# Other PSUM banks for the recurrent block's gate and input tiles, and each modulation tile one place earlier

## The chip, the core and the metric

The kernel runs on one core of a Trainium2 chip. The metric is the device time of one execution in microseconds (us). The core has five engines that run side by side and meet only at semaphores: TensorE (PE, matrix products, with weight loads as PEld), VectorE (DVE), ScalarE (ACT), GpSimd (POOL) and SyncE (SP, which issues most DMAs). PE writes its products into PSUM, which has 8 banks of 128 x 512 fp32 values; DVE and ACT read them there.

## The reference, cut to what matters

Two transformer-like blocks of one layer each run over 512 tokens of width 1024. The first (`first_block`) has latent attention, a Fourier branch, gates and 16 experts. The second (`second_block`) has a gated recurrence, a short convolution and a feed-forward part.

```
mod_l = s_lat @ w_mod + b_mod                 # shift, scale, gate: 6 x 1024
h = modulate(rms(x), sh1, sc1);  p = h @ w_in
ga, gb = sigmoid(p[GA]), sigmoid(p[GB])
x = x + g1 * (ga * (attn @ w_o) + gb * (fourier @ w_fourier)) @ w_out
x = x + g2 * expert_choice(modulate(rms(x), sh2, sc2))
# second block
z = rms(x) @ w_in_2 -> lru_x, lru_gate, sc_b, sc_c, sc_x
lru_x = causal_dwconv(lru_x); r, i = sigmoid(lru_x @ wa), sigmoid(lru_x @ wx)
y_lru = scan(a(r), sqrt(1 - a^2) * i * lru_x) * gelu(lru_gate)
y_sc = sc_b * causal_dwconv(sc_c * sc_x)
x = x + concat(y_lru, y_sc) @ w_out_2
x = x + (gelu(conv(h @ w_gate)) * conv(h @ w_up)) @ w_down;  out = rms(x)
```

## The kernel before

Activations are kept transposed: 128 channels on the partitions, 512 tokens along the free dimension, so that one PSUM bank holds one tile of 128 channels. Each fp32 product of the projections is made of three products: the operands are split into a high and a low part, and `mm3` (lines 959 to 963) issues high x high (L961), low x high (L962) and high x low (L963). `project` runs `mm3` over the contraction blocks, 8 of them for an input of 1024, so a tile is 24 matmuls. Weights arrive in chunks of 128 x 2048; ACT writes their high part (L1704) and POOL their low part (L895).

The order on each engine is the order of the code. Which bank a tile goes to is settled by a plan that is made before the program is built (`make_plan`). Each `p.add(name, by=..., bank=...)` enters a tile in the order in which PE will open it. Its bank is the one given, or the next of the list that the last `p.phase(n, banks)` set. The plan also notes which tile held that bank before, and which event frees it (`by`). On PE, `open_tile` (line 935) waits for that event before the tile's first matmul. So the plan does not move an instruction; it decides what PE waits for at the head of each tile.

Three places matter here.

**Gate projections and modulation.** The tiles `ga` 0 to 7 and `gb` 0 to 7 are projections of 24 matmuls each (lines 1180 to 1185). Between them PE runs `mod_b_tile(k)`, k = 0 to 15: two products with one column, which sum over partitions what DVE has made in `macc`. `mod_b_tile` waits for `macc_done` k + 1 (line 996). On DVE, `modulation_b(c)` (line 2100) multiplies one chunk of modulation weights, 8 instructions long, the last of which (L2112, into `macc`) signals `macc_done`. `modulation_b(0)` starts when the query rows are finished (`qtok_done` 8). DVE does `modulation_b` 0 to 3, and then always one `mod_b_evac(c)` (L2097) and `modulation_b(c + 4)`. In the kernel before, `mod_b` 0 stands behind `ga` 4, `mod_b` 4 behind `gb` 0, and `mod_b` 12 to 15 behind `four_o` 0 to 3.

**Input and gate tiles of the recurrence.** PE makes `lru_x` 0 to 7, each of 24 matmuls, and behind `lru_x` 3, 4, 5, 6 and 7 the small products of the gates (`lru_r` and `lru_i`, lines 1537 and 1540): those of index 0; 1 and 2; 3; 4; 5. Tiles 6 and 7 follow behind `sc_c` 0. DVE takes each `lru_x` with `lru_conv(j)`: L2627, L2633, twice L2636, and L2638, which signals `conv_done` j + 1 and frees the bank of `lru_x` j. Ahead of it, from j = 3, comes `lru_gates(j - 3)` on DVE (L2643), which waits for ACT's sigmoid of `lru_i`.

**The recurrence's output gates and `mix_o`.** PE makes `lru_gate` 0 to 7, one after the other. Each is scaled on DVE (L2689), passed through a gelu on ACT (L2016), multiplied on DVE (L2694), split into its high part on ACT (L1714) and its low part on DVE (L2075), and only this last instruction frees its bank. Then `project_two` opens `mix_o` 0 and `mix_o` 1 together, before the first matmul of either, and runs 12 blocks of both: four of the short convolution, then eight of the recurrence.

In the kernel before `lru_x` 5 goes to the bank of `lru_x` 2, `mix_o` 0 to that of `lru_gate` 2, and `mix_o` 1 to that of `lru_gate` 3.

Of the kernel before, what the change touches and what calls it, by code (L numbers as in the profile page):

```python
# [33 lines left out]
LRU = 8  # L34
# [16 lines left out]
B = 128  # L51
# [151 lines left out]
def blocks(base, first, count, width=B):  # L203

    return range(base + first // CH, base + (first + count * width - 1) // CH + 1)


def split_steps():

    o = Order()  # L210
    for j in range(KD):
        o.add("h", j)
    for j in range(KD):
        o.add("hc", j)
    o.add("f", 0)
    o.add("f", 1)
    for j in range(QL):
        o.add("cq", j)
    for j in range(KL):
        o.add("ckv", j)  # L220
    o.add("f", 2)
    o.add("f", 3)
    for g in range(NF + 1):
        if g < NF:
            o.add("f_ch", g, 0)
            o.add("f_ch", g, 1)
        if g >= 1:
            o.add("four", g - 1)
    for h in range(H):
        o.add("q", h)  # L230
        o.add("k", h, 0)
        o.add("k", h, 1)
    for j in range(4):
        o.add("attn", j)
    for j in range(KD):
        o.add("m", j)
    for i in range(PAIRS):
        o.add("ye", i, 0)
        o.add("ye", i, 1)
    for j in range(KD):  # L240
        o.add("g", j)
    for j in range(SC):
        o.add("y_sc", j)
    for j in range(LRU):
        o.add("y_lru", j)
    for j in range(KD):
        o.add("g2", j)
    for q in range(QUARTERS):
        for i in range(FQ):
            o.add("ff", q, i)  # L250
    return o


SPLITS = split_steps()
# [7 lines left out]
PRE_FF = PRE_SC + SC + LRU  # L262
GATES_AFTER = {3: (0,), 4: (1, 2), 5: (3,), 6: (4,), 7: (5,)}
GATES_LAST = (6, 7)
X_BANKS = (3, 4, 0, 1, 6, 0, 1, 6)
R_BANKS = (2, 2, 3, 2, 2, 2, 2, 3)
I_BANKS = (5, 7, 4, 3, 5, 7, 0, 1)


SQ0 = 5 + QL + KL + 1  # L270
# [10 lines left out]
def make_plan():  # L281
    p = Plan()
# [37 lines left out]
    for half in range(2):  # L320
        for t in range(TT):
            p.add("uq", half, t, by=("qtok_done", half * TT + t + 1), bank=half * TT + t,
                  split=[c for k in range(QL) for c in blocks(s1, q_block(half, k), 1, QW)])
    p.phase(6)
    for j in range(KD):
        p.add("ga", j, by="act", split=blocks(s1, S1_GA + j * 8 * B, 8))
        if j >= 4:
            p.add("mod_b", j - 4, by=("modb_done", j - 3))
    for j in range(KD):
        p.add("gb", j, by="act", split=blocks(s1, S1_GB + j * 8 * B, 8))  # L330
        p.add("mod_b", 4 + j, by=("modb_done", 5 + j))

    def four_o(j, bank=None):
        p.add("four_o", j, by=("resid_done", j + 1), split=blocks(s1, S1_FO[j], NF), bank=bank)

    for j in range(KD // 2):
        four_o(j)
        p.add("mod_b", 12 + j, by=("modb_done", 13 + j))
    for t in range(KT):
        p.add("uk", t, by=("ktok_done", t + 1), split=blocks(s1, S1_K, 8), bank=t)  # L340
    for t in range(KT):
# [80 lines left out]
    w = SPLIT0["w_in_2"]  # L422

    def lru_gates(i):
        p.add("lru_r", i, by="act", bank=R_BANKS[i])
        p.add("lru_i", i, by=("lru_b_done", i + 1), bank=I_BANKS[i])

    for j in range(LRU):
        p.add("lru_x", j, by=("conv_done", j + 1), split=blocks(w, j * 8 * B, 8), bank=X_BANKS[j])
        for i in GATES_AFTER.get(j, ()):  # L430
            lru_gates(i)
    for j in range(SC):
        if j == 1:
            p.phase(6, (2, 0, 3, 1, 4, 5))
        p.add("sc_c", j, split=blocks(w, (LRU + 3 * j) * 8 * B, 8), bank=4 if j == 0 else None)
        if j == 0:
            for i in GATES_LAST:
                lru_gates(i)
        p.add("sc_x", j, split=blocks(w, (LRU + 3 * j + 1) * 8 * B, 8), bank=5 if j == 0 else None)
        p.add("sc_b", j, by=("lo_done", SPLITS["y_sc", j] + 1), split=blocks(w, (LRU + 3 * j + 2) * 8 * B, 8),  # L440
              bank=6 if j == 0 else None)
    for j in range(LRU):
        p.add("lru_gate", j, by=("lo_done", SPLITS["y_lru", j] + 1), split=blocks(w, (LRU + 3 * SC + j) * 8 * B, 8))
    for j in range(KD):
        p.add("mix_o", j, by=("resid_done", RES2 + j + 1), split=blocks(SPLIT0["w_out_2"], j * 12 * B, 12),
              bank=(5, 2, 0, 3, 1, 4, 1, 4)[j])
    w = SPLIT0["ffn"]
    p.phase(5)
    for q in range(QUARTERS):
# [6 lines left out]


PLAN = make_plan()
TILE = PLAN.tiles
LAST = PLAN.last_user  # L460
# [28 lines left out]
def build(nc, stream, cols_d, x_d, ctx_d, router_d, wab_d, rope_d, rope_t_d, rot_d, dftc_d, ident_d, iota_d, xt_d, out):  # L489
    with ExitStack() as ctx:  # L490
        base = 16512

        def at(name, kb, shape, dt=F32):
            return nc.alloc_sbuf_tensor_at(name, shape, dt, offset=base + int(kb * 1024))

        def sem(name):
            return ctx.enter_context(nc.semaphore(name))
# [149 lines left out]
        sc_c = at("sc_c", R + 112, [P, T])  # L647
# [36 lines left out]
        lo_done = sem("lo_done")  # L684
# [5 lines left out]
        modb_done = sem("modb_done")  # L690
# [240 lines left out]
        def _(pe):  # L931
# [33 lines left out]
            def done(ins):  # L965
                ins.then_inc(tile_full, 1)
# [26 lines left out]
            def mod_b_tile(k):  # L993

                o = open_tile("mod_b", k)
                pe.wait_ge(macc_done, k + 1)
                for m in range(2):
                    last = mm(o[:, m:m + 1], macc[:, k % 4, m, :], one, start=True, stop=True)
                done(last)
# [182 lines left out]

            for j in range(KD):
                done(project(open_tile("ga", j), s1, S1_GA + j * 8 * B, B, ks, hx))
                if j >= 4:
                    mod_b_tile(j - 4)
            for j in range(KD):
                done(project(open_tile("gb", j), s1, S1_GB + j * 8 * B, B, ks, hx))
                mod_b_tile(4 + j)
            pe.wait_ge(lo_done, SPLITS["four", NF - 1] + 1)  # L1190

            def four_out(j, behind=None):
# [8 lines left out]

            for j in range(KD // 2):
                four_out(j)
                mod_b_tile(12 + j)

            def token_rows(o, t, off):
                tok = slice(t * P, t * P + P)
# [852 lines left out]
        def _(dve):  # L2060
# [34 lines left out]
            def mod_b_evac(k):  # L2095
                m = 16 + 2 * k
                V.tensor_tensor(mod[:, m:m + 2, 0], take("mod_b", k)[:, 0:2], col("b_mod", m, 2), ALU.add)\  # L2097
                    .then_inc(modb_done, 1)
# [109 lines left out]
            for s in range(2):  # L2208
                w = slice(0, T) if s == 0 else slice(T, TK)
# [48 lines left out]
            for i in range(2):  # L2258
                w = rope_t[:, i * TT:(i + 1) * TT, :]
# [45 lines left out]
            for c in range(5):  # L2305
                mod_b_evac(c)
                modulation_b(c + 4)
            for c in range(5, 12):
                mod_b_evac(c)
                if c + 4 < 16:  # L2310
                    modulation_b(c + 4)
# [6 lines left out]

            for j in range(KD // 2):
                four_gate(j)  # L2320
                mod_b_evac(12 + j)

            V.memset(k_hi[0][QK:QK + 1, :].bitcast(F32), 1.0)
            V.memset(k_lo[0][QK:QK + 1, :].bitcast(F32), 0.0)
# [253 lines left out]
            for i in range(PAIRS):  # L2578
# [24 lines left out]
                for half in range(2):  # L2603
# [5 lines left out]
                    w = slice(half * T, half * T + T)  # L2609
# [93 lines left out]
            for q in range(QUARTERS):  # L2703
                for i in range(FQ + 1):
                    if i < FQ:
# [14 lines left out]
                        if g >= 2:  # L2720
                            p = SPLITS["ff", (g - 2) // FQ, (g - 2) % FQ]
# [173 lines left out]
```

## Time and profile before

| | us |
|---|---|
| median of 3 runs | 1334.85 (1334.09 to 1336.41) |
| the profiled execution, its whole time | 1334.09 |
| its span in the trace | 1332.2 |
| PE busy | 1313.8 (99%) |
| DVE busy | 690.1 (52%) |
| ACT busy | 461.6 (35%) |
| POOL busy | 433.8 (33%) |
| mean granted clock of PE | 0.996 |

The table says that PE hardly ever stands idle. A matmul in this trace is shown with its latency: one of 128 x 512 lasts 0.39 us, but the next starts before it ends. Idle time shorter than that overlap does not show as idle, so starts are to be compared, not busy shares.

### The profile page before, as it was taken

What the parts mean: (1) busy time and instruction counts of PE and PEld (TensorE: products, weight loads), DVE (VectorE), ACT (ScalarE), POOL (GpSimd) and SP (SyncE); (2) the same over time, 40 slices, a digit from 0 to 9 for tenths busy, and PEclk for the clock granted to TensorE, in tenths of its full rate; (3) what the DMA queues carried; (4) which work ended last, traced back from release to release, by engine and by line L of the source; (5) the groups of instructions that cost most, each with busy time, mean ns of one, the idle gap of its engine ahead of it and who ended that gap; (6) DMA issues with size and microseconds to landing.
All of it is one profiled execution on the core that took longest, in us unless ns stands there. A gap on an engine that the chain in (4) does not pass through costs nothing.

```text
span 1332.2 us, 15820 instructions
## 1 busy us (share of the span) xinstructions
PE 1313.8 (99%) x6366; PEld 966.9 (73%) x6366; DVE 690.1 (52%) x1261; ACT 461.6 (35%) x618; POOL 433.8 (33%) x136
## 2 busy tenths in 40 slices
PE   8999999999999899999999999999999999999998
PEld 6789888865587834343457788888888888888887
DVE  2465987757783733343356656612562551551553
ACT  4335223345621221121135571433341431431431
POOL 3143244247612000000015333444245344444440
PEclk9999999999999899999999999999999999999999
DMA  9521198201025799999983122222132223123101
GB/s 378 214 96 64 58 356 336 103 1 64 32 96 189 294 375 421 421 421 420 421 367 127 63 80 110 96 95 95 63 126 98 93 95 118 71 94 126 64 1 64
DMA packets 34501, 226.70 MB, mean 170 GB/s; under 512 B 4064, under 2 KB 4704, under 8 KB 8448
## 3 DMA queue, kind: packets, MB, share of 16 engines
q1 hardware_dynamic: 32992, 218.93, 42.9%
q0 software_dynamic: 1152, 4.19, 0.8%
q10 hardware_dynamic: 288, 2.62, 0.5%
q8 instruction: 48, 0.79, 0.2%
q14 instruction: 21, 0.17, 0.0%
HBM read 221.53 MB, written 4.19 MB: 169 GB/s over the span
## 4 chain that ended last, share of the span: by engine, by line
PE 94%; DVE 3%; DMA 1%; ACT 1%; SPq 0%; issue 0%; DVEq 0%; ACTq 0%
PE psum L961 24%; PE psum L963 23%; PE psum L962 23%; PE psum L1465 13%; DMA mod_in<-in_stream 1%; PE psum L1273 1%; PE psum L1239 1%; PE psum L1450 1%; PE psum L1453 1%; PE psum L1008 1%; PE psum L1537 1%; PE psum L1425 1%; PE psum L1674 1%; DVE rs L2381 1%; PE psum L1013 0%; DVE work L2512 0%
## 5 line engine op out<-in xcount | busy, mean ns | idle before, releaser
L895 POOL TENSOR_TENSOR w_lo<-raw,w_hi 128x2048 fp32r<-128x2048 f32 x79 | 365.3, 4627 | 589.9 <-ACT w_hi L1704 589.9
L961 PE MATMUL psum<-b_hi,w_hi 128*128 128x512 f32 x608 | 238.1, 392 | 0.1
L963 PE MATMUL psum<-b_hi,w_lo 128*128 128x512 f32 x608 | 236.7, 389 | 0.0
L962 PE MATMUL psum<-b_lo,w_hi 128*128 128x512 f32 x608 | 236.6, 389 | 0.0
L1704 ACT ACTIVATE w_hi<-raw 128x2048 fp32r<-128x2048 f32 x80 | 152.6, 1907 | 145.4 <-PE psum L963 101.9
L961 PEld LDWEIGHTS psum<-b_hi,w_hi 128*128 128x128 f32 x608 | 114.1, 188 | 30.6 <-issue 5.7
L963 PEld LDWEIGHTS psum<-b_hi,w_lo 128*128 128x128 f32 x608 | 114.1, 188 | 23.9
L962 PEld LDWEIGHTS psum<-b_lo,w_hi 128*128 128x128 f32 x608 | 114.2, 188 | 23.4
L1465 PE MATMUL psum<-ex_ring,xe 128*64 128x512 f32 x488 | 108.8, 595 | 0.9 <-ACT xe L1929 0.9
L2429 DVE TENSOR_TENSOR x<-psum,x 128x512 f32<-128x512 f32 x40 | 27.4, 691 | 124.3 <-PE psum L963 124.3
L961 PE MATMUL psum<-h_hi,w_hi 128*128 128x512 f32 (+1 forms) x208 | 84.7, 407 | 1.3 <-POOL w_lo L878 1.3
L1465 PEld LDWEIGHTS psum<-ex_ring,xe 128*64 128x64 f32 x488 | 34.1, 137 | 66.3 <-issue 65.4
L963 PE MATMUL psum<-h_hi,w_lo 128*128 128x512 f32 (+1 forms) x208 | 81.8, 393 | 0.0
L962 PE MATMUL psum<-h_lo,w_hi 128*128 128x512 f32 (+1 forms) x208 | 81.7, 393 | 0.0
L961 PE MATMUL psum<-ff_hi,w_hi 128*128 128x512 f32 x192 | 74.7, 389 | 0.0
L962 PE MATMUL psum<-ff_lo,w_hi 128*128 128x512 f32 x192 | 74.7, 389 | 0.0
L963 PE MATMUL psum<-ff_hi,w_lo 128*128 128x512 f32 x192 | 74.7, 389 | 0.0
L2710 DVE TENSOR_TENSOR psum<-psum,rstd_s 128x512 f32<-128x512 f32 x48 | 33.5, 697 | 77.4 <-PE psum L963 77.4
L905 POOL DMA_INDIRECT xg<-xt,ids x8 | 8.3, 1040 | 189.6 <-DVE ids L2539 139.0
L2431 DVE SCALAR_TENSOR_TENSOR x<-psum,mod,x 128x512 f32<-128x512 f32 x72 | 51.0, 743 | 25.6 <-PE psum L963 21.0
L1929 ACT ACTIVATE xe<-psum,mod,small 128x128 f32<-128x128 f32 x64 | 23.9, 459 | 83.7 <-PE psum L1425 83.7
L1465 PE MATMUL psum<-ex_ring,act_e 128*64 128x512 f32 x224 | 49.7, 595 | 0.7 <-DVE act_e L2597 0.7
(419 smaller groups left out, 2290.9 us busy)
## 6 DMA issues: line engine op xcount, KB each, us to landing
raw<-in_stream SPq DMA_DIRECT2D x97, 1024.0 KB, 4.8
ex_ring<-in_stream SPq DMA_DIRECT2D x89, 1024.0 KB, 17.7
mod_in<-in_stream SPq DMA_DIRECT2D x8, 1024.0 KB, 21.0
ex_last<-in_stream SPq DMA_DIRECT2D x7, 1024.0 KB
x<-in_x SPq DMA_DIRECT2D x4, 512.0 KB, 6.0
x<-in_x ACTq DMA_DIRECT2D x1, 2048.0 KB, 7.4
xt<-h2t SPq DMA_DIRECT2D x8, 256.0 KB, 11.7
out<-y_out SPq DMA_DIRECT2D x8, 256.0 KB, 3.3
```

Source lines behind the costliest of these rows:

```text
L895: nc.gpsimd.tensor_tensor(w_lo[:, slot, :], raw[:, raw_slot, :], w_hi[:, slot, :].bitcast(F32), ALU.subtract).then_inc(w_lo_done, 1)
L961: mm(o, w[0], x[0], start=start, stop=False)
L962: mm(o, w[0], x[1], start=False, stop=False)
L963: return mm(o, w[1], x[0], start=False, stop=stop)
L1008: mm(psum[:, bank, 0:P], ones[:], ones[:], start=True, stop=True)
L1239: done(mm(o[:, 0:KH], q_hi[b][0:QK, q * P:(q + 1) * P], k_hi[b][0:QK, s * KH:(s + 1) * KH], start=True, stop=True))
L1465: last = mm(o[e * CAP:(e + 1) * CAP, :], x_of(k, e), w[:, (2 * (k - k0) + e) * T:(2 * (k - k0) + e + 1) * T], start=k == 0, stop=k == ks - 1)
L1704: A(w_hi[:, c % NHL, :], raw[:, n % NRAW, :], ACT.Copy).then_inc(w_hi_done, 1)
L1929: ins = A(xe[:, i % 2, k, :], o[:, j * P:(j + 1) * P], ACT.Identity, bias=mod[:, 3 * KD + k, 0:1], scale=a2[:, k:k + 1])
L2429: ins = V.tensor_tensor(x1[:, j, :], o, x1[:, j, :], ALU.add)
L2431: ins = V.scalar_tensor_tensor(out=x1[:, j, :], in0=o, scalar=scale, in1=x1[:, j, :], op0=ALU.mult, op1=ALU.add)
L2710: V.tensor_tensor(o, o, rstd, ALU.mult).then_inc(ffz_done, 1)
```

## The change

Two things change. First, in the gate stage every `mod_b` tile stands one place earlier: `mod_b` 0 behind `ga` 3, `mod_b` 4 behind `ga` 7, `mod_b` 5 + j behind `gb` j, and `mod_b` 13 to 15 behind `four_o` 1 to 3. DVE's `mod_b_evac(12)` accordingly stands ahead of `four_gate(0)`. Second, the banks of the recurrence's tiles no longer come from hand-written lists but, from `lru_x` 2 on, from a rotation over all eight banks (0, 1, 2, 5, 6, 7, 3, 4), which also serves the short convolution and `lru_gate`. `mix_o` gets the banks 0, 1, 2, 3, 4, 5, 4, 5.

```
@@ make_plan
     for j in range(KD):
         p.add("ga", j, by="act", split=blocks(s1, S1_GA + j * 8 * B, 8))
-        if j >= 4:
-            p.add("mod_b", j - 4, by=("modb_done", j - 3))
+        if j >= 3:
+            p.add("mod_b", j - 3, by=("modb_done", j - 2))
     for j in range(KD):
         p.add("gb", j, by="act", split=blocks(s1, S1_GB + j * 8 * B, 8))
-        p.add("mod_b", 4 + j, by=("modb_done", 5 + j))
+        p.add("mod_b", 5 + j, by=("modb_done", 6 + j))
     for j in range(KD // 2):
         four_o(j)
-        p.add("mod_b", 12 + j, by=("modb_done", 13 + j))
+        if j >= 1:
+            p.add("mod_b", 12 + j, by=("modb_done", 13 + j))
...
-X_BANKS = (3, 4, 0, 1, 6, 0, 1, 6)
-R_BANKS = (2, 2, 3, 2, 2, 2, 2, 3)
-I_BANKS = (5, 7, 4, 3, 5, 7, 0, 1)
     def lru_gates(i):
-        p.add("lru_r", i, by="act", bank=R_BANKS[i])
-        p.add("lru_i", i, by=("lru_b_done", i + 1), bank=I_BANKS[i])
+        p.add("lru_r", i, by="act")
+        p.add("lru_i", i, by=("lru_b_done", i + 1))
     for j in range(LRU):
-        p.add("lru_x", j, by=("conv_done", j + 1), split=blocks(w, j * 8 * B, 8), bank=X_BANKS[j])
+        if j == 2:
+            p.phase(8, (0, 1, 2, 5, 6, 7, 3, 4))
+        p.add("lru_x", j, by=("conv_done", j + 1), split=blocks(w, j * 8 * B, 8), bank=3 + j if j < 2 else None)
     for j in range(SC):
-        if j == 1:
-            p.phase(6, (2, 0, 3, 1, 4, 5))
-        (sc_c, sc_x, sc_b 0 in banks 4, 5, 6)
+        (sc_c, sc_x, sc_b from the rotation)
     for j in range(KD):
         p.add("mix_o", j, ...,
-              bank=(5, 2, 0, 3, 1, 4, 1, 4)[j])
+              bank=(0, 1, 2, 3, 4, 5, 4, 5)[j])
@@ PE
             for j in range(KD):
                 done(project(open_tile("ga", j), s1, S1_GA + j * 8 * B, B, ks, hx))
-                if j >= 4:
-                    mod_b_tile(j - 4)
+                if j >= 3:
+                    mod_b_tile(j - 3)
             for j in range(KD):
                 done(project(open_tile("gb", j), s1, S1_GB + j * 8 * B, B, ks, hx))
-                mod_b_tile(4 + j)
+                mod_b_tile(5 + j)
             for j in range(KD // 2):
                 four_out(j)
-                mod_b_tile(12 + j)
+                if j >= 1:
+                    mod_b_tile(12 + j)
@@ DVE
-            for c in range(5, 12):
+            for c in range(5, 13):
                 mod_b_evac(c)
             for j in range(KD // 2):
                 four_gate(j)
-                mod_b_evac(12 + j)
+                if j >= 1:
+                    mod_b_evac(12 + j)
```

What the plan makes of it at the places where a tile's bank was last held by something recent (tile: who had its bank before, and what frees it):

| tile | before | after |
|---|---|---|
| `lru_x` 5 | `lru_x` 2, `conv_done` 3 | `lru_x` 3, `conv_done` 4 |
| `lru_x` 6 | `lru_x` 3, `conv_done` 4 | `lru_x` 4, `conv_done` 5 |
| `lru_x` 7 | `lru_x` 4, `conv_done` 5 | `lru_r` 2, ACT |
| `sc_x` 0 | `lru_i` 4 | `lru_x` 7, `conv_done` 8 |
| `lru_gate` 6 | `lru_gate` 0 | `sc_x` 3 |
| `lru_gate` 7 | `lru_gate` 1 | `sc_b` 3 |
| `mix_o` 0 | `lru_gate` 2 | `lru_gate` 6 |
| `mix_o` 1 | `lru_gate` 3 | `lru_gate` 7 |

On PE, at the boundary between `ga` 3 and `ga` 4, the kernel before reads as follows. The row with a wait is the first matmul of `ga` 4.

```order
L963 MATMUL psum<-h_hi,w_lo 128x512
L961 MATMUL psum<-h_hi,w_hi 128x512
L962 MATMUL psum<-h_lo,w_hi 128x512
L963 MATMUL psum<-h_hi,w_lo 128x512
L961 MATMUL psum<-h_hi,w_hi 128x512 [waits qtok_done]
L962 MATMUL psum<-h_lo,w_hi 128x512
```

The changed kernel has the two products of `mod_b` 0 there (its lines are numbered 3 lower).

```order
L960 MATMUL psum<-h_hi,w_lo 128x512
L958 MATMUL psum<-h_hi,w_hi 128x512
L959 MATMUL psum<-h_lo,w_hi 128x512
L960 MATMUL psum<-h_hi,w_lo 128x512
L995 MATMUL psum<-ones,macc 128x1 [waits macc_done,qtok_done]
L995 MATMUL psum<-ones,macc 128x1
L958 MATMUL psum<-h_hi,w_hi 128x512 [waits qtok_done]
```

So PE meets the wait for the first `macc` at the end of `ga` 3, 24 matmuls earlier than before, and all of `ga` 4 is queued behind it. On DVE the end of the modulation work reads so before (L2317 is `four_gate`, L2097 `mod_b_evac`):

```order
L2112 SCALAR_TENSOR_TENSOR macc<-raw,small,psum 128x256 [waits dve_seq]
L2317 TENSOR_TENSOR gbf<-psum,gbf 128x512 [waits freed_act,tile_full]
L2097 TENSOR_TENSOR mod<-psum,cols 128x2 [waits tile_full]
L2317 TENSOR_TENSOR gbf<-psum,gbf 128x512 [waits freed_act,tile_full]
L2097 TENSOR_TENSOR mod<-psum,cols 128x2 [waits tile_full]
```

In the changed kernel it reads:

```order
L2110 SCALAR_TENSOR_TENSOR macc<-raw,small,psum 128x256 [waits dve_seq]
L2095 TENSOR_TENSOR mod<-psum,cols 128x2 [waits tile_full]
L2315 TENSOR_TENSOR gbf<-psum,gbf 128x512 [waits freed_act,tile_full] x2
L2095 TENSOR_TENSOR mod<-psum,cols 128x2 [waits tile_full]
L2315 TENSOR_TENSOR gbf<-psum,gbf 128x512 [waits freed_act,tile_full]
```

One evacuation has moved ahead of the first `four_gate`. Everywhere else the instructions of every engine stand in the order of before.

## Rows read from the trace of the kernel before

**Rows 1.** The page, part 4: the chain that ended last, by engine and by line.

```profile
PE 94%; DVE 3%; DMA 1%; ACT 1%; SPq 0%; issue 0%; DVEq 0%; ACTq 0%
PE psum L961 24%; PE psum L963 23%; PE psum L962 23%; PE psum L1465 13%; DMA mod_in<-in_stream 1%; PE psum L1273 1%; PE psum L1239 1%; PE psum L1450 1%; PE psum L1453 1%; PE psum L1008 1%; PE psum L1537 1%; PE psum L1425 1%; PE psum L1674 1%; DVE rs L2381 1%; PE psum L1013 0%; DVE work L2512 0%
```

**Rows 2.** Timeline (start, duration, what) of PE: end of `ga` 3, then `mod_b` 0.

```profile
159.70 0.39 PE L963 MATMUL psum<-h_hi,w_lo 128*128 128x512 f32 x1
159.93 0.39 PE L961 MATMUL psum<-h_hi,w_hi 128*128 128x512 f32 x1
...
165.37 0.50 PE L998 MATMUL psum<-ones,macc 128*128 128x1 f32 x4
```

**Rows 3.** Timeline of DVE ahead of the first two `macc`.

```profile
152.41 4.12 DVE L2294 TENSOR_TENSOR q_tok<-q_tok,q_sw 128x128 f32<-128x128 f32 x1
...
157.68 0.29 DVE L2294 TENSOR_TENSOR q_tok<-q_tok,q_sw 128x128 f32<-128x128 f32 x1
...
162.41 0.48 DVE L2112 SCALAR_TENSOR_TENSOR macc<-raw,small,psum 128x256 f32<-128x256 f32 x1
...
166.47 0.48 DVE L2112 SCALAR_TENSOR_TENSOR macc<-raw,small,psum 128x256 f32<-128x256 f32 x1
```

**Rows 4.** Timeline of POOL in that stretch.

```profile
151.72 4.66 POOL L895 TENSOR_TENSOR w_lo<-raw,w_hi 128x2048 fp32r<-128x2048 f32 x1 [2.07 <-ACT w_hi L1704]
```

**Rows 5.** Timeline of PE: first matmuls of `lru_x` 5 and `lru_x` 6.

```profile
727.07 0.50 PE L961 MATMUL psum<-b_hi,w_hi 128*128 128x512 f32 x1
...
733.75 0.50 PE L961 MATMUL psum<-b_hi,w_hi 128*128 128x512 f32 x1
```

**Rows 6.** Timeline of DVE: convolutions of `lru_x` 3 and 4.

```profile
723.96 1.81 DVE L2643 TENSOR_TENSOR lru_b<-lru_b,conv_u 128x512 f32<-128x512 f32 x1 [0.65 <-ACT lru_b L1980]
725.69 0.69 DVE L2627 TENSOR_TENSOR psum<-psum,rstd_s 128x512 f32<-128x512 f32 x1
...
728.83 0.75 DVE L2638 SCALAR_TENSOR_TENSOR conv_u<-psum,cols,conv_u 128x509 f32<-128x509 f32 x1
729.49 0.68 DVE L2643 TENSOR_TENSOR lru_b<-lru_b,conv_u 128x512 f32<-128x512 f32 x1
...
733.24 0.75 DVE L2638 SCALAR_TENSOR_TENSOR conv_u<-psum,cols,conv_u 128x509 f32<-128x509 f32 x1
```

**Rows 7.** Timeline of PE: last matmul of `lru_gate` 7, first of `mix_o`.

```profile
857.99 0.39 PE L963 MATMUL psum<-b_hi,w_lo 128*128 128x512 f32 x1
858.22 0.39 PE L961 MATMUL psum<-ysc_hi,w_hi 128*128 128x512 f32 x1
```

**Rows 8.** Timeline of DVE: `lru_gate` 7 from its scaling to its low part.

```profile
858.42 0.70 DVE L2689 TENSOR_TENSOR psum<-psum,rstd_s 128x512 f32<-128x512 f32 x1 [2.79 <-PE psum L963]
...
860.99 0.69 DVE L2694 TENSOR_TENSOR psum<-psum,lru_v 128x512 f32<-128x512 f32 x1
862.35 0.69 DVE L2075 TENSOR_TENSOR ylru_lo<-psum,ylru_hi 128x512 fp32r<-128x512 f32 x1 [0.67 <-ACT ylru_hi L1714]
```

**Rows 9.** The chain in order of time: DVE frees PE.

```profile
692.28 0.76 DVE b_lo L2465
693.09 0.50 PE psum L961
```

**Rows 10.** Timeline of PE around 85 us: after one-column products.

```profile
83.65 1.50 PE L1131 MATMUL psum<-ones,sqk 32*128 32x1 f32 x12
...
85.67 0.63 PE L962 MATMUL psum<-h_lo,w_hi 128*128 128x512 f32 x1
...
88.23 0.48 PE L962 MATMUL psum<-h_lo,w_hi 128*128 128x512 f32 x1
```

**Rows 11.** Windows: length, busy of PE, PEld, DVE, ACT, POOL; PE clock; DMA.

```profile
83.00:90.00 7.00, 7.00 (x34) 5.98 (x34) 2.47 (x15) 1.03 (x1) 4.54 (x1) 0.76 0.39 142
452.00:457.00 5.00, 3.19 (x26) 2.66 (x24) 3.52 (x11) 0.00 (x0) 0.00 (x0) 1.00 1.02 392
456.00:465.00 9.00, 8.96 (x50) 8.63 (x50) 7.37 (x30) 0.00 (x0) 2.69 (x2) 0.62 0.55 176
```

More of the change, by code:

```diff
@@ L432, in make_plan @@
     for j in range(SC):
-        if j == 1:
-            p.phase(6, (2, 0, 3, 1, 4, 5))
-        p.add("sc_c", j, split=blocks(w, (LRU + 3 * j) * 8 * B, 8), bank=4 if j == 0 else None)
+        p.add("sc_c", j, split=blocks(w, (LRU + 3 * j) * 8 * B, 8))
         if j == 0:
@@ L438, in make_plan @@
                 lru_gates(i)
-        p.add("sc_x", j, split=blocks(w, (LRU + 3 * j + 1) * 8 * B, 8), bank=5 if j == 0 else None)
-        p.add("sc_b", j, by=("lo_done", SPLITS["y_sc", j] + 1), split=blocks(w, (LRU + 3 * j + 2) * 8 * B, 8),
-              bank=6 if j == 0 else None)
+        p.add("sc_x", j, split=blocks(w, (LRU + 3 * j + 1) * 8 * B, 8))
+        p.add("sc_b", j, by=("lo_done", SPLITS["y_sc", j] + 1), split=blocks(w, (LRU + 3 * j + 2) * 8 * B, 8))
     for j in range(LRU):
```

## The prediction

> **What bounds the kernel now.** I read the chain that ended last first, in the page [rows 1]: it runs over PE for 94% of the span. So the kernel is a queue of matmuls, and the question for any change is how long PE stands. No instruction's work changes here, only what PE waits for at the head of some tiles and where 16 small tiles stand. I then went tile by tile: in the timeline of PE, the time at which each moved or rebanked tile is opened; in that of DVE or ACT, the time at which its new release happens. The reader should see, for each pair, which of the two is later. Since starts of 128 x 512 matmuls are 0.23 us apart while each is shown for 0.39 us [rows 2], I compare starts. In the same views PE has no gap longer than that overlap at any of these places in the kernel before, so there is no wait of size for the change to remove; nor can the DVE work that ends the modulation stage earlier by one evacuation give PE anything, since no matmul stands still for it.
>
> **First term: `mod_b` 0.** Before, it starts at 165.37 behind `ga` 4. Now it is due behind `ga` 3, where `ga` 4's first matmul started: 159.93 [rows 2]. It needs the first `macc`, written at 162.41 + 0.48 = 162.89 [rows 3]. DVE is late there because it is itself busy with the query rows and then with eight instructions of modulation; nothing in the change starts them earlier. From the end of a DVE instruction to the matmul it releases takes 693.09 - (692.28 + 0.76) = 0.05 us [rows 9]. So PE stands from 159.93 to 162.94: **3.0 us**. `ga` 4 and everything after it is queued behind. Bounds: one 128 x 128 instruction of DVE lasts 4.12 us where its like lasts 0.29, and ends as POOL's 151.72 + 4.66 ends [rows 3, 4]; had it not been held, the first `macc` would have come 3.8 us earlier and the wait would be nothing. That is the lower end, 0; the upper is 3.5, with the 0.50 us of the small products themselves no longer overlapped [rows 2]. I take 3.0, since the row is a measurement of just this. The next one, `mod_b` 1, comes at about 162.94 + 5.4 + 0.5 = 168.8, after its `macc` of 166.47 + 0.48 = 166.95 [rows 3]: no second wait, and the later ones have more room, because from here PE is 3 us later and DVE is not.
>
> **Second term: `lru_x` 5.** PE opens it at 727.07 [rows 5]. Its bank was that of `lru_x` 2 and becomes that of `lru_x` 3, whose convolution ends at 728.83 + 0.75 = 729.58 [rows 6]. With 0.05 us to release: 729.63 - 727.07 = **2.6 us**. Bounds: the L2643 ahead of that convolution takes 1.81 us, its next like 0.68 [rows 6]; without that 1.1 us the wait is 1.4. Above, 3.0, if DVE's order slips as much as between such rows. I take 2.6.
>
> **Third term: `mix_o` 0 and 1.** Both are opened before the first matmul, at 858.22 [rows 7]. Their banks become those of `lru_gate` 6 and 7. `lru_gate` 7 is only just finished: DVE begins it at 858.42 after waiting for PE, and its low part ends at 862.35 + 0.69 = 863.04 [rows 8]. Before, PE filled this time with the blocks of the short convolution, and the last block of `lru_gate` 7 was not needed until 22 blocks of 0.68 us later. Now it stands until 863.09: **4.9 us**. DVE waited 2.79 us for PE at this point [rows 8], so DVE is not behind and the length does not depend on the other two terms. Bounds 4.4 (the in-between L2694 of tile 6 out of the way) to 5.3.
>
> **What I cost at nothing.** `lru_x` 6 takes the bank of `lru_x` 4, freed at 733.24 + 0.75 = 733.99 [rows 6]; PE would open it at 733.75 [rows 5], but is 2.6 us later by then, so there are 2.3 us of room, and a wait of 0.3 us only if the second term were missing. The other new owners in the recurrence, the short convolution and `lru_gate` were released 4 us or more ahead of their next tile, with a whole tile of 24 matmuls between, or by an event for which that tile waits anyway (`lru_i` 2). `lru_gate` 6 and 7 get banks free far earlier than before, but did not wait for the old ones. From `ff_g` 0 on the banks are as before.
>
> Sum of the waits: 3.0 + 2.6 + 4.9 = 10.5 us. PE carries them to the end, because what follows on other engines starts from PE's results.
>
> **The clock after a wait.** The granted clock falls in this trace to its half level (1.2 GHz) after two thin stretches of PE: at about 85 us, right after a run of one-column products, matmuls start (88.23 - 85.67) / 6 = 0.43 us apart instead of 0.23 [rows 10]; by the mean of 0.76 over 7 us this lasts 3.4 us [rows 11]. The second follows a stretch in which PE is busy for 3.19 of 5 us, and with a mean of 0.62 over 9 us lasts 6.8 us [rows 11]. A fall of the first kind costs 3.4 x (1 - 0.23 / 0.43) = 1.6 us. No row shows PE waiting 3 to 5 us with nothing to do, so this is bounded by 0 and by three falls, 4.8 us. The third wait is longer than the thin stretch of 85 us and wholly empty, so I count one fall there; for the two shorter ones together I count half a fall: 1.5 x 1.6 = **2.4 us**.
>
> The Trainium skill (TensorE: Matmul & The Clock Gate, section "HAM oscillation — how this bites in real kernels") says that an idle gap that is long enough puts the clock back to half, and that the burst behind it then starts cold. By that rule alone I would expect a fall behind the third wait and none behind the two shorter ones, 1346.6 by the sum below. Rows 10 and 11 go further, since there the clock fell although PE was at work.
>
> **The sum.** The profiled execution took 1334.09 us, 1.89 more than its span. 1334.09 + 10.5 + 2.4 = 1347.0. The median of the runs lies 0.8 us higher than that execution; whether this is a matter of the clock I can't tell, so I take the middle of 1347.0 and 1347.8 and predict **1347.4 us**.
>
> **Rivals.**
> 1. *The waits without the clock.* An empty wait leaves the clock alone. For it: no row shows such a wait being punished. Against it: rows 10 and 11. 1334.09 + 10.5 = 1344.6, 1345.4 beside the median. Chance 0.15.
> 2. *One of the two shorter waits is not there*, because DVE comes in time: for `mod_b` 0 if the hold beside POOL is shorter, for `lru_x` 5 if L2643 is not drawn out. Against it: both depend on instructions that the change leaves where they are. Without the first: 1334.09 + 7.5 + 1.6 = 1343.2; without the second about the same. Chance 0.09.
> 3. *More falls.* Each wait halves the clock, or one fall lasts as long as the 6.8 us one: 1334.09 + 10.5 + 4.8 = 1349.4, up to 1351 with both. Chance 0.18.
> 4. *Not slower: PE's delay is given back.* The one place where PE could regain it is a stretch in which it is paced by transfers: there a late PE would find its weights waiting and stand less. The price to regain is 10.5 us at least, and it decides from the point where transfers, not PE, set the pace. Against it: the chain has 1% of DMA, and that for `mod_in`, the modulation weights of the program's first stage [rows 1], long ahead of the first wait. Even the gate stage, where weights come latest, has PE without gaps. 1334 us. Chance 0.03. That the plan's waits are not carried out as I read them is contained in this.
>
> **How the numbers follow.** The forecast, three waits and one or two falls, has 0.55; the rivals 0.15, 0.09, 0.18 and 0.03. Its own range is 1345.5 to 1349. The range for 8 in 10 reaches down to 1342.5, which takes in a missing short wait, and up to 1351. About 0.2% (2.7 us) can be told from no change; every case but the last is above 1340. Faster 0.01, the same 0.02, slower 0.97.
>
> **What would show it.** In the changed kernel's trace PE should list waits of about 3.0 us for DVE's `macc` near 160 us, 2.6 us for DVE's `conv_u` near 727 + 3 us, and 4.9 us for DVE's `ylru_lo` near 858 + 6 us or later. Behind the last, the clock should stand at half for 3.4 us, with matmuls 0.43 us apart. Elsewhere, PE's starts should be shifted and otherwise the same. I would be wrong if the second or third wait were missing from the list, if PE now waited for weights behind `ga` 4, or if the shift between the two traces shrank again anywhere behind 165 us.

## The result and the profile after

The changed kernel took 1351.97 us (median of 4 runs, 1350.67 to 1354.24) against 1335.36 us (median of 4 runs) for the kernel before: ratio 1.0127, 95% interval 1.0109 to 1.0144. That is 1.0 us above the upper end of the predicted range, 1342.5 to 1351 us, and 4.6 us above the forecast of 1347.4. A second series of the same kernel on another chip (`e_again` below) gave 1350.16 us and 1.0102 [1.0087, 1.0118]. The profiled execution took 1351.49 us, its span is 1349.6 us, so 17.4 us more than the 1332.2 of before.

From the page of the changed kernel, its span, PE's busy time and the chain that ended last, which answer to [rows 1]:

```profile
span 1349.6 us, 15820 instructions
...
PE 1319.4 (98%) x6366; PEld 970.1 (72%) x6366; DVE 691.6 (51%) x1261; ACT 461.7 (34%) x618; POOL 433.2 (32%) x136
...
PE 91%; DVE 5%; ACT 1%; issue 1%; DMA 1%; POOL 0%; SPq 0%; DVEq 0%; ACTq 0%
```

There are as many instructions as before. PE's busy time grew by 5.6 us, though it does no more work, and its share of the span fell. So two things must be found: where PE stands still, and where it works slowly. For the first, the waits of PE in the changed kernel (what is waited for; us in total, times, longest us). I show the four with the longest single wait:

```profile
PE psum L958 <- DVE ylru_lo L2073: 4.8, 1, 4.8
PE psum L995 <- DVE macc L2110: 3.0, 1, 3.0
PE psum L958 <- DVE conv_u L2637: 2.5, 1, 2.5
...
PE psum L1398 <- DVE work L2511: 1.8, 1, 1.8
```

The first three are new and are those of the three terms; the fourth is in the kernel before with the same 1.8 us. The lines have moved up by 3 or less: L958 to L960 here are L961 to L963 of before. The matmuls at these places answer to [rows 2], [rows 5] and [rows 7]. Timeline of PE in the changed kernel, end of `ga` 3, `mod_b` 0 and `ga` 4:

```profile
160.13 0.39 PE L960 MATMUL psum<-h_hi,w_lo 128*128 128x512 f32 x1
163.47 0.58 PE L995 MATMUL psum<-ones,macc 128*128 128x1 f32 x4 [2.95 <-DVE macc L2110]
163.90 0.48 PE L958 MATMUL psum<-h_hi,w_hi 128*128 128x512 f32 x1
...
165.61 0.63 PE L958 MATMUL psum<-h_hi,w_hi 128*128 128x512 f32 x1
166.04 0.63 PE L959 MATMUL psum<-h_lo,w_hi 128*128 128x512 f32 x1
```

The last gate product ahead of `lru_x` 5, and `lru_x` 5, in the changed kernel:

```profile
731.77 0.59 PE L1538 MATMUL psum<-conv_u,wab 64*64 64x512 f32 x1
734.86 0.60 PE L958 MATMUL psum<-b_hi,w_hi 128*128 128x512 f32 x1 [2.50 <-DVE conv_u L2637]
...
735.68 0.63 PE L960 MATMUL psum<-b_hi,w_lo 128*128 128x512 f32 x1
736.11 0.63 PE L958 MATMUL psum<-b_hi,w_hi 128*128 128x512 f32 x1
```

The same gate product in the kernel before:

```profile
726.55 0.59 PE L1540 MATMUL psum<-conv_u,wab 64*64 64x512 f32 x1
```

The last matmul of `lru_gate` 7 and the first of `mix_o` in the changed kernel:

```profile
867.39 0.39 PE L960 MATMUL psum<-b_hi,w_lo 128*128 128x512 f32 x1
872.53 0.76 PE L958 MATMUL psum<-ysc_hi,w_hi 128*128 128x512 f32 x1 [4.75 <-DVE ylru_lo L2073]
...
873.51 0.63 PE L960 MATMUL psum<-ysc_hi,w_lo 128*128 128x512 f32 x1
873.94 0.63 PE L958 MATMUL psum<-ysc_hi,w_hi 128*128 128x512 f32 x1
```

Behind each wait there is a stretch in which matmuls start 0.43 us apart, as in [rows 10], instead of 0.23: at once behind the second and third, and behind the first only from 165.2 us on, 1.7 us after its end. The windows say the same (length; busy us of PE, PEld, DVE, ACT, POOL; PE's granted clock, DMA share, GB/s). First the changed kernel, then the one before, in the same four stretches:

```profile
160.00:171.00 11.00, 8.05 (x31) 6.25 (x30) 8.38 (x18) 0.60 (x1) 0.00 (x0) 0.84 0.59 214
437.00:470.00 33.00, 29.42 (x212) 26.65 (x212) 23.03 (x74) 7.48 (x13) 2.62 (x2) 0.90 0.77 285
730.00:741.00 11.00, 8.50 (x39) 5.52 (x38) 9.52 (x13) 5.43 (x8) 0.45 (x1) 0.84 0.28 98
861.00:880.00 19.00, 14.25 (x51) 11.21 (x51) 5.68 (x9) 6.24 (x7) 9.95 (x3) 0.82 0.35 119
```

```profile
160.00:171.00 11.00, 11.00 (x52) 9.15 (x51) 9.62 (x21) 0.60 (x1) 0.00 (x0) 1.00 0.61 220
437.00:470.00 33.00, 28.85 (x209) 25.19 (x211) 26.65 (x99) 9.76 (x20) 2.69 (x2) 0.90 0.82 307
730.00:741.00 11.00, 11.00 (x55) 7.31 (x54) 10.68 (x15) 6.89 (x9) 4.64 (x1) 1.00 0.05 10
861.00:880.00 19.00, 19.00 (x86) 15.73 (x85) 3.49 (x6) 6.58 (x7) 5.55 (x2) 1.00 0.21 76
```

A mean of 0.84 over 11 us is 2 x 0.16 x 11 = 3.5 us at 1.2 GHz; 0.82 over 19 us is 6.8 us. Before, all three of these stretches have 1.00, and the router's stretch (437 to 470 us) has 0.90, which is 6.6 us, in both. The stretch at 85 us has 0.76 in both, too.

Now the start of one and the same matmul in both traces gives the whole account, from the rows above and [rows 2, 5, 7]:

| place | before | after | shift | growth since the line above |
|---|---|---|---|---|
| last matmul of `ga` 3 | 159.70 | 160.13 | 0.43 | |
| first of `ga` 4 | 159.93 | 163.90 | 3.97 | 3.11 wait, 0.43 `mod_b` 0 itself |
| last gate product ahead of `lru_x` 5 | 726.55 | 731.77 | 5.22 | 1.25 = 1.68 slow, less the 0.43, which before came later |
| `lru_x` 5 | 727.07 | 734.86 | 7.79 | 2.57 wait |
| last of `lru_gate` 7 | 857.99 | 867.39 | 9.40 | 1.61 slow |
| `mix_o` 0 | 858.22 | 872.53 | 14.31 | 4.91 wait |
| end | 1332.2 | 1349.6 | 17.4 | 3.09 slow |

Waits 10.6 us, slow matmuls 6.4 us, and 0.43 us that was there before the first wait: 17.4 us.

### The profile page after: what moved, and what is told of

It is laid out like the page before. It is cut to its first block, busy times and chain, and to the rows that moved or that the text cites. A ratio compares the mean times of both kernels' runs of the same rounds, so it can differ in the third digit from the quotient of the medians.

```text
span 1349.6 us, 15820 instructions
## 1 busy us (share of the span) xinstructions
PE 1319.4 (98%) x6366; PEld 970.1 (72%) x6366; DVE 691.6 (51%) x1261; ACT 461.7 (34%) x618; POOL 433.2 (32%) x136
## 4 chain that ended last, share of the span: by engine, by line
PE 91%; DVE 5%; ACT 1%; issue 1%; DMA 1%; POOL 0%; SPq 0%; DVEq 0%; ACTq 0%
PE psum L958 23%; PE psum L960 22%; PE psum L959 22%; PE psum L1463 12%; PE psum L1271 1%; PE psum L1237 1%; PE psum L1448 1%; PE psum L1451 1%; DVE q_tok L2292 1%; DMA x<-in_x 1%; PE psum L1423 1%; PE psum L1005 1%; PE psum L1672 1%; DVE rs L2380 0%; PE psum L1010 0%
## 5 line engine op out<-in xcount | busy, mean ns | idle before, releaser
L958 PE MATMUL psum<-b_hi,w_hi 128*128 128x512 f32 x608 | 238.7, 393 | 2.7 <-DVE conv_u L2637 2.5
L960 PE MATMUL psum<-b_hi,w_lo 128*128 128x512 f32 x608 | 237.3, 390 | 0.0
L958 PEld LDWEIGHTS psum<-b_hi,w_hi 128*128 128x128 f32 x608 | 114.6, 188 | 33.6 <-issue 4.9
L960 PEld LDWEIGHTS psum<-b_hi,w_lo 128*128 128x128 f32 x608 | 114.6, 188 | 23.9
L958 PE MATMUL psum<-h_hi,w_hi 128*128 128x512 f32 (+1 forms) x208 | 85.2, 410 | 1.3 <-POOL w_lo L875 1.3
L960 PE MATMUL psum<-h_hi,w_lo 128*128 128x512 f32 (+1 forms) x208 | 82.7, 398 | 0.0
L958 PE MATMUL psum<-ff_hi,w_hi 128*128 128x512 f32 x192 | 74.7, 389 | 0.0
L960 PE MATMUL psum<-ff_hi,w_lo 128*128 128x512 f32 x192 | 74.7, 389 | 0.0
```

Source lines behind the costliest of these rows:

```text
L958: mm(o, w[0], x[0], start=start, stop=False)
L960: return mm(o, w[1], x[0], start=False, stop=stop)
```

## The experiments

Theory A: each of the three waits costs its length and, behind it, a stretch at half clock, and nothing else changed. Rivals: the slow stretches are chance and have nothing to do with the waits; the change costs elsewhere; the terms don't add. The series were run beside the kernel before, whose median was 1336.75 (21 runs), 1336.20 (15), 1336.87 (21) and 1336.96 us (17). The ratio and its interval are those on record; they are not exactly the quotient of the two medians shown (`e_banks` 1.0075 against 1.0086, `e_mix` 1.0048 against 1.0053), so differences of 1 us between two ways of reckoning mean nothing here.

| run | median us | ratio, 95% interval |
|---|---|---|
| `e_mod` | 1339.48 | 1.0020 [1.0011, 1.0030] |
| `e_x5` | 1340.05 | 1.0029 [1.0019, 1.0038] |
| `e_mix` | 1343.80 | 1.0048 [1.0034, 1.0062] |
| `e_mix6` | 1340.09 | 1.0020 [1.0009, 1.0030] |
| `e_mixfill` | 1340.02 | 1.0026 [1.0016, 1.0035] |
| `e_again` | 1350.16 | 1.0102 [1.0087, 1.0118] |
| `e_filled` | 1354.31 | 1.0125 [1.0109, 1.0140] |
| `e_filled2` | 1345.46 | 1.0061 [1.0047, 1.0074] |
| `e_banks` | 1347.70 | 1.0075 [1.0061, 1.0089] |
| `e_mixfix` | 1343.16 | 1.0047 [1.0033, 1.0061] |
| `e_more` | 1335.06 | 0.9988 [0.9978, 0.9998] |
| `e_more2` | 1333.16 | 0.9976 [0.9965, 0.9987] |

**Each part alone.** `e_mod` is the kernel before with the modulation tiles one place earlier.

```
-        if j >= 4:
-            p.add("mod_b", j - 4, by=("modb_done", j - 3))
+        if j >= 3:
+            p.add("mod_b", j - 3, by=("modb_done", j - 2))
```

> The kernel before with the modulation tiles one place earlier and nothing else. Theory A (each new wait costs its length and, behind it, a stretch at the half granted clock): 3.0 us of waiting for macc plus 3.4 us at half, 1.6 us, so 4.6 us over the kernel before; in the trace one stretch at half right behind the wait. Theory B (the waits cost their length only, and the rest of the 17 us comes from elsewhere): 3.0 us, and no new stretch at half near 165 us.

`e_x5` is the kernel before with the bank of `lru_x` 3 given to `lru_x` 5.

```
-X_BANKS = (3, 4, 0, 1, 6, 0, 1, 6)
+X_BANKS = (3, 4, 0, 1, 6, 1, 0, 6)
-I_BANKS = (5, 7, 4, 3, 5, 7, 0, 1)
+I_BANKS = (5, 7, 4, 3, 5, 7, 1, 0)
```

> The kernel before with lru_x 5 in the bank of lru_x 3 (and lru_x 6 in that of lru_x 2); nothing else is changed. Theory A: 2.5 us of waiting for conv_u plus one stretch at half, 1.6 us: 4.1 us over the kernel before. Theory B: 2.5 us.

`e_mix` is the kernel before with `mix_o` 0 and 1 in the banks of `lru_gate` 6 and 7.

```
-              bank=(5, 2, 0, 3, 1, 4, 1, 4)[j])
+              bank=(1, 4, 5, 2, 0, 3, 0, 3)[j])
```

> The kernel before with mix_o 0 and 1 in the banks of lru_gate 6 and 7; nothing else is changed. Theory A: 4.8 us of waiting plus a stretch at half of 3.4 to 6.8 us, 1.6 to 3.2 us: 6.4 to 8.0 us over the kernel before. Theory B: 4.8 us.

The waits, from the timelines of PE. `e_mod`:

```profile
163.74 0.47 PE L999 MATMUL psum<-ones,macc 128*128 128x1 f32 x3 [2.94 <-DVE macc L2114]
```

The list of waits of `e_x5`:

```profile
PE psum L961 <- DVE conv_u L2638: 2.5, 1, 2.5
```

`e_mix`:

```profile
865.20 0.76 PE L961 MATMUL psum<-ysc_hi,w_hi 128*128 128x512 f32 x1 [4.75 <-DVE ylru_lo L2075]
```

Each has its own wait, within 0.1 us of its length in the changed kernel, and none of the others. The clock of the stretch around it, `e_mod`, `e_x5` and `e_mix` in turn:

```profile
160.00:171.00 11.00, 8.06 (x40) 6.54 (x39) 9.46 (x20) 0.60 (x1) 0.00 (x0) 1.00 0.61 209
```

```profile
730.00:741.00 11.00, 9.93 (x39) 7.15 (x40) 8.29 (x13) 5.78 (x8) 0.56 (x1) 0.84 0.08 33
```

```profile
861.00:880.00 19.00, 14.80 (x53) 12.02 (x54) 2.77 (x5) 3.58 (x4) 4.55 (x1) 0.82 0.28 108
```

So the clock did not fall behind the 2.9 us wait of this execution of `e_mod`. It did for 3.5 us behind the 2.5 us wait of `e_x5`, and for 6.8 us behind the 4.8 us wait of `e_mix`. The three ratios add up to 1.0097, 13.0 us, against 1.0127 and 1.0102 for the whole. That leaves 0.7 us by the second series of the whole, and 4.0 us by the first. So the parts add up to the second; what made the first 3.3 us longer no run shows.

**A shorter wait at the same place.** In `e_mix6` only `lru_gate` 6 has to be out before `mix_o` 0.

```
-              bank=(5, 2, 0, 3, 1, 4, 1, 4)[j])
+              bank=(1, 5, 4, 2, 0, 3, 0, 3)[j])
```

> The kernel before with one difference: the first tile of mix_o takes the bank of lru_gate 6 instead of that of a block of the short convolution; lru_gate 7's bank goes to the second tile's place no more. So PE should stand about 2.9 us ahead of mix_o instead of the 4.8 us of the run with both banks. Theory A (a wait costs its length, and a stretch at half clock behind it that is longer the longer the wait): +2.9 us and one short stretch of 3.4 us at half, +1.6 us, so 0.2 to 0.4% over the kernel before. Rival B (what costs is the place: whatever empty wait stands at mix_o gives 6.8 us at half): +2.9 +3.2 = 6.1 us, 0.45%. Rival C (a wait under 3 us leaves the clock alone): +2.9 us, 0.2%.

PE's wait and the stretch around it:

```profile
863.51 0.50 PE L961 MATMUL psum<-ysc_hi,w_hi 128*128 128x512 f32 x1 [2.75 <-DVE ylru_lo L2075]
```

```profile
861.00:880.00 19.00, 16.49 (x66) 13.49 (x67) 3.09 (x5) 3.58 (x4) 4.59 (x1) 0.91 0.31 111
```

0.91 over 19 us is 3.4 us at half: half as long as in `e_mix`, at the same place. Against `e_mix` the time fell by 0.0028 of 1336.9, 3.7 us, for a wait shorter by 2.0 us; the halved stretch gives the other 1.6. The rival that the place decides is refuted. That a wait under 3 us leaves the clock alone is refuted by this trace for this execution; the ratio alone (2.7 us over the kernel before) fits it better than theory A (4.5 us).

**The waits filled with idle products.** If the clock falls because PE has nothing to do, it should stay up when PE multiplies ones by ones meanwhile; these products' results are not used. `e_filled` is the changed kernel with 26, 22 and 42 such products ahead of the three waits; `e_filled2` has 13, 11 and 20.

```
                 o = open_tile("mod_b", k)
+                if k == 0:
+                    idle_products(13, PLAN.bank[TILE["mod_b", 0]])
...
+                if j == 5:
+                    pe.wait_ge(freed_act, PLAN.freed_count(TILE["lru_r", 0]))
+                    idle_products(11, PLAN.bank[TILE["lru_r", 0]])
...
+            pe.wait_ge(lo_done, SPLITS["y_lru", 0] + 1)
+            idle_products(20, PLAN.bank[TILE["lru_gate", 0]])
             project_two((open_tile("mix_o", 0), open_tile("mix_o", 1)),
```

> The changed kernel with products of ones (26, 22 and 42 of 128 x 128, about 0.11 us each) that PE runs while it waits at the three places; the waits and everything behind them stay. Theory A: the clock is not halved behind them, so only the waits are left: 10.4 us over the kernel before, 6 us under the changed kernel, and no stretch at half near 165, 735 and 872 us. Theory B: no different from the changed kernel, about 1352 us.

> The changed kernel with 13, 11 and 20 products of ones run by PE inside the three waits (each such product is two instructions of 0.114 us, so 3.0, 2.5 and 4.6 us of filling; the first try had twice as many and was as long as its filling). Theory A: the waits stay, the half clock behind them goes: 10.4 to 10.9 us over the kernel before, and 4 to 6 us under the changed kernel; no stretch at half near 165, 735 and 872 us. Theory B: the same as the changed kernel.

`e_filled` failed as a test of the time, by an error of size: such a product is two matmuls and two weight loads, so the filling was twice as long as I had reckoned. `e_filled2` at `mix_o`:

```profile
866.88 4.62 PE L1007 MATMUL psum<-ones 128*128 128x128 f32 x40
871.79 0.47 PE L958 MATMUL psum<-ysc_hi,w_hi 128*128 128x512 f32 x1 [0.29 <-DVE ylru_lo L2080]
872.10 0.39 PE L959 MATMUL psum<-ysc_lo,w_hi 128*128 128x512 f32 x1
872.33 0.40 PE L960 MATMUL psum<-ysc_hi,w_lo 128*128 128x512 f32 x1
```

20 products are 40 matmuls in 4.62 us, 0.115 us each, and end 0.3 us before `mix_o` starts. Behind them matmuls start 0.23 us apart at once. The clock around the three places in `e_filled2`:

```profile
160.00:170.00 10.00, 10.00 (x60) 8.71 (x59) 8.63 (x18) 0.60 (x1) 0.00 (x0) 1.00 0.48 179
729.00:739.00 10.00, 10.00 (x63) 7.38 (x62) 9.12 (x12) 7.16 (x11) 2.31 (x1) 1.00 0.30 107
865.00:878.00 13.00, 12.71 (x76) 11.13 (x76) 3.29 (x5) 3.58 (x4) 6.03 (x2) 1.00 0.25 88
```

`e_filled`, too, has 1.00 at all three. Beside the changed kernel on the same chip, `e_again`, `mod_b` 0 and `mix_o` start as long after they are due (3.0 and 4.9 us), the filling ahead of `lru_x` 5 ends within 0.2 us of the tile's release, and the time is 1350.16 - 1345.46 = 4.7 us lower, 5.5 us by the ratios. That is what the clock behind the waits costs, measured by taking it away, as far as the falls elsewhere are the same in both.

`e_again` is the changed kernel without an edit.

> The changed kernel itself, so that it is timed beside the single parts. Theory A: the sum of the three parts alone (2.7, 3.3 and 7.0 us measured) plus what a second and third stretch at half adds, 13 to 17 us over the kernel before. Theory B (the parts add up and nothing else): 13.0 us.

Its list of waits has the same three, 4.8, 3.0 and 2.5 us. Its profiled execution shows 0.84 in 160 to 171 us and 0.82 in 861 to 880 us, but behind `lru_x` 5's wait this:

```profile
730.00:741.00 11.00, 8.50 (x49) 5.02 (x45) 9.85 (x15) 6.40 (x9) 0.00 (x0) 1.00 0.27 98
```

So the fall behind a wait of 2.5 us is there in one execution of this kernel and not in another.

`e_mixfill` is `e_mix` with 20 idle products ahead of `mix_o`, in the bank of `lru_gate` 2.

```
+            pe.wait_ge(lo_done, SPLITS["y_lru", 2] + 1)
+            idle_products(20, PLAN.bank[TILE["lru_gate", 2]])
```

> The kernel before with mix_o 0 and 1 in the banks of lru_gate 6 and 7 and 20 products of ones in the wait. Theory A: 4.9 us over the kernel before (7.0 without the products), no stretch at half behind it. Theory B: 7.0 us as without them.

Its clock from 861 to 880 us is 1.00:

```profile
861.00:880.00 19.00, 18.71 (x103) 16.12 (x102) 3.29 (x5) 3.58 (x4) 6.20 (x2) 1.00 0.33 118
```

By the ratios it lies 0.0022, 2.9 us, below `e_mix`; the 6.8 us at half should cost 6.8 x (1 - 0.23 / 0.43) = 3.2 us.

The rival that the slow stretches are chance can be counted out over all profiled executions. In the three windows (160 to 171, 730 to 741, 861 to 880 us) the mean clock is 1.00 in all 21 cases in which the execution does not have that wait, below 1.00 in 12 of the 14 in which it has it unfilled, and 1.00 in all 7 in which it is filled.

**Parts taken out of the change.** `e_banks` is the changed kernel with the modulation tiles where they were (the first diff above, backwards).

> The changed kernel with the modulation tiles back in their old places (banks alone changed). Theory A: 2.5 + 4.8 us of waits and two or three stretches at half of 3.4 us, 1.6 us each: 10.5 to 12.1 us over the kernel before, and 3 to 4.6 us under the changed kernel. Theory B: 7.3 us over the kernel before.

`e_mixfix` is the changed kernel without the wait at `mix_o`.

```
-              bank=(0, 1, 2, 3, 4, 5, 4, 5)[j])
+              bank=(2, 5, 3, 4, 0, 1, 3, 4)[j])
```

> The changed kernel with the banks of mix_o alone chosen so that neither lru_gate 6 nor lru_gate 7 has to be out before its first tiles; modulation tiles and recurrence banks stay as changed. Theory A: the 4.8 us wait and the 6.8 us at half behind it (3.2 us lost) go, 8.0 us in all; the two short waits of 3.0 and 2.5 us stay. From the two series of the changed kernel (1.0127 and 1.0102 of the kernel before) that leaves 1.004 to 1.007. Rival (the terms do not add, another wait takes the place of the one removed): over 1.008.

`e_banks` waits 4.8 and 2.5 us, and has 0.82 and 0.84 behind them; it came out at 1.0075. `e_mixfix` waits 2.9 and 2.5 us, has 0.84 behind both and 1.00 from 861 to 880 us, and 1.0047 is in the range of theory A, not of the rival. No wait took the place of a removed one in either.

**The times against what was expected.** In us over the kernel before, by the ratios:

| run | theory A | its rival | measured, 95% interval |
|---|---|---|---|
| `e_mod` | 4.6 | 3.0 | 2.7 [1.5, 4.0] |
| `e_x5` | 4.1 | 2.5 | 3.9 [2.5, 5.1] |
| `e_mix` | 6.4 to 8.0 | 4.8 | 6.4 [4.5, 8.3] |
| `e_mix6` | 4.5 | 2.9 or 6.1 | 2.7 [1.2, 4.0] |
| `e_mixfill` | 4.9 | 7.0 | 3.5 [2.1, 4.7] |
| `e_again` | 13 to 17 | 13.0 | 13.6 [11.6, 15.8] |
| `e_filled2` | 10.4 to 10.9 | as `e_again` | 8.2 [6.3, 9.9] |
| `e_banks` | 10.5 to 12.1 | 7.3 | 10.0 [8.2, 11.9] |
| `e_mixfix` | 5.3 to 9.4 | over 10.7 | 6.3 [4.4, 8.2] |

No run lies above theory A, and five lie 0.5 to 2.2 us below it. In `e_mod` and `e_mix6` the rival that gives the clock no price is nearer, though the profiled execution of `e_mix6` shows the fall (that of `e_mod` does not). So the waits and the falls behind them are shown by the traces; that the falls cost time is shown by the two pairs with and without filling, and a single short wait is too small a part for it. Why the times are short of theory A stays open. One rival was not tested: the shift may take falls away elsewhere. In the 11 executions of `e_mod` the mean clock is 0.9944, against 0.9936 in the 21 of the kernel before beside it, although a wait was added.

**A version faster than both.** In the router the kernel before already runs idle products while DVE picks tokens, but they end early: PE is busy for 3.19 of 5 us and the clock falls behind it, to a mean of 0.62 from 456 to 465 us [rows 11]. `e_more` has seven more.

```
-            idle_products(38, 6)
+            idle_products(45, 6)
```

> The kernel before with 45 instead of 38 idle products of ones in the router's stretch near 455 us, where the clock fell to half for 6.8 us in the profiled execution of the kernel before; they fill the part of PE's wait for DVE that was left empty. Theory A (a clock that falls behind thin stretches of PE): if those seven keep it up, the 6.8 us at half shrink to 3.4 or 0, 1.6 to 3.2 us faster than the kernel before (0.1 to 0.25%). Rival (that stretch's fall comes from the small products ahead of it, not from the empty rest): same time within 0.1%, half level there as before.

> The kernel with 45 idle products a second time, since its gain over the kernel before (0.9988 [0.9978, 0.9998], 1.6 us) was near to what can be told from nothing, and its profiled execution happened to have no half-clock stretch even at 85 us, where the edit changes nothing. Theory A (the filled place keeps the clock up in the router's stretch): 0.997 to 1.000 again, and less time at half between 437 and 470 us in the profiled execution than the 6.8 us of the kernel before. Rival (chance of the executions): 1.000 or over, with 6.8 us or more at half there.

The wait that ends the filling, in the timeline of PE; first before, then `e_more`:

```profile
454.74 0.42 PE L1400 MATMUL psum<-ident,work 16*128 16x16 f32 x4 [1.77 <-DVE work L2512]
```

```profile
453.74 0.42 PE L1400 MATMUL psum<-ident,work 16*128 16x16 f32 x4 [0.21 <-DVE work L2512]
```

The same 9 us, 456 to 465, in `e_more` and in `e_more2`:

```profile
456.00:465.00 9.00, 7.11 (x56) 6.67 (x58) 7.74 (x35) 1.78 (x6) 2.25 (x2) 1.00 0.49 155
```

```profile
456.00:465.00 9.00, 7.88 (x62) 7.30 (x61) 7.25 (x30) 0.22 (x1) 2.26 (x2) 1.00 0.55 178
```

Both profiled executions keep the full clock from 437 to 470 us. Of this only the part behind the filling, from 452 us on, can be the work of the edit; ahead of it the profiled execution of the kernel before has 1.00, too. From 452 to 470 us all twelve profiled executions without the seven products have a fall, and its length goes with the wait that ends the filling: 6.8 us at half in the four with a wait for `work` of 1.4 to 1.8 us (the kernel before, the changed kernel, `e_x5`, `e_banks`), 3.2 to 4.3 us in the eight with 0.3 to 0.7 us, none in the two of `e_more` and `e_more2` with 0.2 us. Over all executions the mean clock rose from 0.9935 to 0.9963 in the one series and from 0.9932 to 0.9969 in the other. The gain is 1.6 and 3.2 us by the ratios; the first is barely clear of nothing, the second clear. This is the fastest kernel of the study.

## Why the prediction was right or wrong

- **First, second and third term: right.** Predicted 3.0, 2.6 and 4.9 us, measured 3.11, 2.57 and 4.91 between starts. Each could be read off the trace of before, as the time of the release less the time at which the tile is due, since on both engines the work ahead of it stayed where it was.
- **What I cost at nothing: right.** No other new wait of size is in the list, and the shift never shrank. 0.43 us were lost ahead of the first wait, where the change edits nothing. Of these 0.36 are there by 49 us (the same small products, L989 before and L986 after, start at 49.64 instead of 49.28), and PE's waits for ACT's first squares in the first 12 us came to 2.5 instead of 0.7 us. In the other runs, which edit nothing there either, they came to 1.1 to 2.9 us, so this is scatter.
- **The clock after a wait: this step failed.** The mechanism was named, but the term was sized wrongly: I counted 2.4 us, the profiled execution has 6.4 (1.7, 1.6 and 3.1). The 4.0 us between them, the 0.43 us of scatter and 0.1 us in the waits are the 4.5 us by which this execution exceeded the sum of 1347.0. There were two errors in it. I took one fall to last 3.4 us also behind the third wait, although [rows 11] had both lengths, 3.4 and 6.8 us; in all four profiled executions with the 4.8 us wait (the change twice, `e_mix`, `e_banks`) it lasted 6.8 us. And I gave the two short waits half a fall together; a fall of 3.4 us stands behind the first in 3 of 4 executions (not in `e_mod`) and behind the second in 4 of 5 (not in `e_again`). By these counts the term is (3/4 + 4/5) x 1.6 + 3.2 = 5.7 us, and the runs with filled waits measured 4.7 (5.5 by the ratios). With 5.7, the sum would have been 1334.09 + 10.5 + 5.7 = 1350.3 us. The third rival, more falls, gave 1349.4 and up to 1351; it was the right mechanism and should have been the forecast, and the first series lies 1 us above even that.
- **The rule of the skill.** The Trainium skill (TensorE: Matmul & The Clock Gate, section "HAM oscillation — how this bites in real kernels") ties the fall to an idle gap that is long enough, and I had read from it one fall, behind the third wait alone. The runs agree for that wait (6.8 us at half behind 4.8 us in 4 of 4 executions) and go further: 8 of the 10 unfilled waits of 2.5 to 3.0 us were followed by half clock, too.
- **The sum: its base was a lucky execution.** The profiled one of before has a mean clock of 0.996. In its 74 executions of the four later series the kernel before ran at 0.991 to 0.997, and the time goes with it: median 1338.05 us in the 6 at 0.991, 1333.43 in the 7 at 0.997. I had left open whether the 0.8 us between the profiled execution and the median were a matter of the clock; they are of the size that this gives. Beside the first series the kernel before took 1335.36 us, 0.9 more than the 1334.5 on which the forecast stood; this is the smaller part of the miss.
- **The rivals.** Waits without the clock is refuted: 10.5 us over the kernel before timed beside it would be 1345.9 us in the first series and 1346.7 in the second, against 1351.97 and 1350.16 measured, while `e_filled2`, from which the falls were taken, lies at 1345.5. A missing short wait is refuted by the list of waits, and a delay given back by the shift, which grew at every line of the table. *What stays open:* the two series of the changed kernel, 1.0127 and 1.0102, have intervals that overlap by little, and the second is 13.6 us where its 10.3 us of waits and the falls in its trace (3.4 and 6.8 us at half, 4.8 us lost) would give 15. The falls at 85 us and in the router, which come and go in every kernel, would be enough to make such a difference, but no run separated them.

## What to carry to other kernels

A wait on a saturated TensorE can cost more than its length: by the traces 4.8 us cost 8, and 2.5 us cost 4.1 where the clock fell behind it; the times came out at 6.4 and 3.9 us. So add a half-clock stretch for each, and look in several profiled executions at whether it is there and how long it lasts. When tiles share PSUM banks, compare when the old tile's last reader ends with when the new tile is due, tile by tile; this rotation gave away the newest, least finished bank just where two stages meet. If a wait can't be avoided, idle products in it that end just before the release kept the clock here, at no price that these runs could tell; in `e_filled`, twice as long as the waits, they cost 8.6 us (1.0125 against 1.0061).

## What the runs showed of the hardware that I had not expected

- The half-clock stretch behind an empty wait has steps: 3.4 us behind 2.5 to 3.0 us (or none, behind 2 of the 10 such waits, `e_mix6` counted), 6.8 us behind 4.8 us. `e_mix6` and `e_mix` show both lengths at the same place in the program.
- The kernel falls to half clock at about 85 us and between 437 and 470 us by itself, not the same way in each execution: `e_more` has 1.00 from 83 to 90 us and `e_more2`, the same program, 0.76. The time goes with the mean clock from 1333 to 1338 us, so such falls are likely to make most of the scatter; that it is these two places was not shown.
- Seven more idle products, 14 matmuls of 0.115 us, in a place where PE waited anyway made the kernel faster by 1.6 and 3.2 us in two series. The stretch at half behind that place was 6.8 us long behind waits of 1.4 to 1.8 us, about half as long behind 0.3 to 0.7 us, and gone at 0.2 us.
- An fp32 product of ones, 128 x 128, runs as two matmuls of 0.115 us with a weight load each.
